# Down weights of experts 3 to 30 as one transfer of 4 MB, on one buffer that is waited for and freed as a whole

## The reference, cut to what matters

```python
def expert_block(args):
    xb, e = args                                   # a block of tokens of expert e
    h = xb @ w_gu[e] + b_gu[e]                     # (1024, 2048) weights: 8 MB
    h_glu = jnp.minimum(h[:, :D_EXPERT], SWIGLU_LIMIT)
    h_lin = jnp.clip(h[:, D_EXPERT:], -SWIGLU_LIMIT, SWIGLU_LIMIT)
    act = h_glu * jax.nn.sigmoid(SWIGLU_ALPHA * h_glu) * (h_lin + 1.0)
    return act @ w_dn[e] + b_dn[e]                 # (1024, 1024) weights: 4 MB
...
return jnp.einsum('tkd,tk->td', y, gates).reshape(bsz, seq, d)
```

## Time and profile before

| | |
|---|---|
| median of the runs | 1021.99 us |
| the profiled execution | 1020.78 us, of which 1019.0 us are its span |
| TensorE (PE) busy | 824.2 us, 81% |
| VectorE busy | 246.4 us, 24% |
| DMA | 421.69 MB, 414 GB/s over the span, about 428 GB/s from 130 us to the end |
| chain that ended last | DMA 56%, PE 36%, VectorE 5% |
| `gu_buf` from `w_gate_up` | 128 transfers of 2048 KB |
| `dn_buf` from `w_down` | 62 transfers of 2048 KB, 2 of 1024 KB |

### The profile page before, as it was taken

How to read it: one execution, slowest core, us unless ns; L and a number is a source line. 1 busy time by engine, 2 the same in 40 slices (tenths; PEclk the granted TensorE clock), 3 DMA queues, 4 the chain that set the end, 5 groups by cost and what they waited for, 6 DMA issues and landing times.

```text
span 1019.0 us, 20186 instructions
## 1 busy us (share of the span) xinstructions
PE 824.2 (81%) x8447; PEld 355.9 (35%) x8448; DVE 246.4 (24%) x692; ACT 79.5 (8%) x184; POOL 7.2 (1%) x25
## 2 busy tenths in 40 slices
PE   9999879898659999985699976666865885965995
PEld 7884433333213334331133421221321332311432
DVE  2473711221112222221112211111111221210233
ACT  1040100000000000000000000000000000000010
POOL 1000000000000000000000000000000000000000
PEclk9999989999899999998799998888989799988989
DMA  9988699999999999999999999999999999999996
GB/s 327 408 355 346 266 425 425 428 428 428 428 429 428 429 428 429 428 429 429 428 429 429 428 428 429 428 429 428 428 430 428 429 429 428 429 428 428 428 428 291
DMA packets 38903, 421.69 MB, mean 414 GB/s; under 512 B 5907, under 2 KB 6347, under 8 KB 14309
## 3 DMA queue, kind: packets, MB, share of 16 engines
q1 hardware_dynamic: 36436, 420.89, 98.0%
q10 hardware_dynamic: 2400, 0.44, 0.2%
q0 software_dynamic: 48, 0.09, 0.0%
HBM read 420.27 MB, written 1.18 MB: 414 GB/s over the span
## 4 chain that ended last, share of the span: by engine, by line
DMA 56%; PE 36%; DVE 5%; issue 2%; SPq 0%; DVEq 0%; POOLq 0%; ACT 0%; POOL 0%
DMA dn_buf<-in_w_down_dram 56%; PE ps L1038 12%; PE ps L1005 12%; PE ps L838 5%; PE ps L886 3%; PE ps L999 2%; PE ps L857 1%; DVE act_t L730 1%; DVE lin L725 1%; DVE lin L728 1%; DVE glu L722 1%; DVE lin L723 1%; DMA gu_buf<-in_w_in_dram 1%; PE ps L918 0%; PE ps L873 0%
## 5 line engine op out<-in xcount | busy, mean ns | idle before, releaser
L1005 PE MATMUL ps<-gu_buf,rows_t 128*32 128x512 f32 x2880 | 363.8, 651 | 102.0 <-DMA gu_buf<-in_w_gate_up_dram 102.0
L1005 PEld LDWEIGHTS ps<-gu_buf,rows_t 128*32 128x32 f32 x2880 | 93.8, 115 | 362.6 <-issue 196.0
L1038 PE MATMUL ps<-dn_buf,act_t 128*32 128x256 f32 x2848 | 171.1, 385 | 52.1 <-DMA dn_buf<-in_w_down_dram 44.1
L722 DVE TENSOR_SCALAR glu<-ps 128x256 f32<-128x256 f32 x45 | 19.1, 425 | 605.2 <-PE ps L1005 605.2
L1038 PEld LDWEIGHTS ps<-dn_buf,act_t 128*32 128x32 f32 x2848 | 87.7, 110 | 123.4 <-DMA dn_buf<-in_w_down_dram 59.2
L999 PE MATMUL ps<-turned,bias_sel 128*32 128x512 f32 x360 | 50.2, 630 | 22.6 <-issue 22.6
L449 ACT ACTIVATE sig<-glu 128x256 f32<-128x256 f32 x45 | 18.8, 417 | 529.1 <-DVE glu L722 529.1
L838 PE MATMUL ps<-turned,gu_buf 128*128 128x256 f32 x256 | 55.7, 379 | 0.0
L979 PE MATMUL ps<-mix,back 32*128 32x256 f32 x720 | 52.2, 404 | 0.5 <-ACT mix L453 0.5
L955 PE MATMUL ps<-xs,onehot 128*32 128x256 f32 x736 | 50.5, 394 | 1.5 <-DVE onehot L709 1.5
L838 PEld LDWEIGHTS ps<-turned,gu_buf 128*128 128x128 f32 x256 | 48.6, 190 | 6.9 <-issue 0.4
(11 more groups left out here) (234 smaller groups left out, 301.6 us busy)
## 6 DMA issues: line engine op xcount, KB each, us to landing
gu_buf<-in_w_gate_up_dram SPq DMA_DIRECT2D x128, 2048.0 KB, 30.2
dn_buf<-in_w_down_dram SPq DMA_DIRECT2D x62, 2048.0 KB, 13.3
gu_buf<-in_w_in_dram SPq DMA_DIRECT2D x4, 2048.0 KB, 18.4
gu_buf<-in_w_out_dram SPq DMA_DIRECT2D x2, 2048.0 KB, 16.9
dn_buf<-in_w_down_dram SPq DMA_DIRECT2D x2, 1024.0 KB, 27.1
xs<-in_x_dram SPq DMA_DIRECT2D x2, 512.0 KB, 5.4
gu_buf<-in_w_in_dram SPq DMA_DIRECT2D x2, 512.0 KB, 6.5
gu_buf<-in_w_in_dram SPq DMA_DIRECT2D x1, 1024.0 KB, 9.6
```

Of the source, the lines that this page charges most:

```text
L722: V.tensor_scalar(glu[:], half(HB, 0), SWIGLU_LIMIT, None, ALU.min).then_inc(S["glu_ok"], 1)
L1005: ins = T.matmul(ps[SLOTS * j:SLOTS * (j + 1), HB, :], rows_t[:, k, :], gu_buf[:, b, k, :].rearrange("p (two n) -> p two n", two=2)[:, :, ...
L1038: ins = T.matmul(ps[SLOTS * j:SLOTS * (j + 1), YB, 0:QF], act_t[:, DK * m + q, :], weights[q][:, QF * j:QF * (j + 1)], start=(m == 0 and q ...
```

## The change

For experts 3 to 30 `stream_dn` waits once, for the second half of the last block of the expert before (`dn_used[DC - 1]`, which is `y_ps`), and issues one transfer for the whole of `dn_buf`: 4 MB, 32 KB per partition. It counts on `dn_in[0]`. On TensorE the first half of the down product waits for that count as before, which now stands for all 4 MB; the second half waits for a count on `dn_in[1]` that has been reached since expert 2 (48), and so no longer waits. The transfers of experts 0 to 2 and 31 are as they were; for expert 31 the count on `dn_in[1]` is a smaller number, since fewer transfers have counted there.

```diff
             def stream_dn(e):
-                used = blocks_before(e)
-                for c in range(DC):
-                    stream_dn_chunk(e, c, used)
+                sp.wait_ge(dn_used[DC - 1], blocks_before(e))
+                sp.dma_start(dn_buf[:].rearrange("p q n -> p (q n)"), dn_src[bass.ds(e, 1)].rearrange("o p r -> p (o r)")).then_inc(dn_in[0], 16)
...
             def pair_of_experts(pair):
                 for b in range(2):
                     e = pair * 2 + b
-                    expert(e, b, (pair + 1) * 16, [down_at(0, e * 16), down_at(1, (e + 1) * 16)])
+                    expert(e, b, (pair + 1) * 16, [down_at(0, e * 16), down_at(1, 48)])
...
             e = E - 2
-            expert(e, 0, 16 * (E // 2), [down_at(0, e * 16), down_at(1, (e + 1) * 16)])
+            expert(e, 0, 16 * (E // 2), [down_at(0, e * 16), down_at(1, 48)])
...
                     elif q == DK:
-                        pe.wait_ge(dn_in[1], 16 * E)
+                        pe.wait_ge(dn_in[1], 64)
```

## The result

The changed kernel takes 1048.51 us (median of 4 runs, 1046.84 to 1049.15), the kernel before on the same chip 1021.94 us. The ratio is 1.0253 (95% interval 1.024 to 1.0266): 26.6 us slower. The forecast was 1033 us with a range up to 1041. The direction was right; of the size the forecast had 11 us.

A forecast was written before the change was run, and what follows sets the result against it. The expert loop was taken as bound by transfer bytes over rate. On the profiled 1020.78 us, +13.3 for the clock and -2.0 for packets gave 1032.1, with the median 1.2 above: 1033 us, range 1021 to 1041.

The forecast's parts named there:

- What bounds the kernel, and where the down weights are issued: Expert loop: transfer bytes over rate, 29.36 us per expert; two-block experts' down issue moves from L + 14.4 to L + 17.9.
- L: The time at which the whole of an expert's down weights has landed; issue times are counted from it.
- The room at full clock: Two-block experts: down issue against the end of the stream in flight, -0.7 to +0.8 us, taken as 0.
- two pieces: Down transfers: issue to first bytes, 0.9 to 1.4 us; last byte to landing, 0 to 1 us.
- rival 3: All 14 two-block experts: issue late at full clock too, room -0.7, 1043 us; chance of above 1037 us 0.14.
- its sign: Transfer queue: gaps also where both experts have two blocks would show the issue late at full clock.
- The Trainium skill's fixed cost of about 2 us: Each DMA transfer: about 2 us beside its bytes; serial it would save 56 us, but taken as overlapped.
- The clock behind the longer wait: TensorE behind one-block experts: half clock after the landing, 1.9 us lost in 7 two-block experts, 13.3 us (0 to 22).
- Larger packets: 28 down transfers with 32 KB per partition, not 16: 2.0 us saved, between 0 and 2.5.
- Fewer issues: SyncE: 28 issues and waits fewer, worth nothing because it waits anyway.

The follow-up runs named there:

- the run with four matmuls: The control with 4 matmuls of 128 x 512 inside its TensorE branch, result not needed: 1036.73 us.
- the control: The changed kernel plus an empty TensorE branch ahead of the act_t wait, taken in the first block behind a one-block expert: 1045.9 us.
- the run with the late release alone: The kernel before, with both 2 MB down transfers issued only when the second half of the expert before is done: 1031.17 us, ratio 1.0077.
- four row groups left out: The changed kernel without four of the eight row groups (k = 0, 2, 4, 6) of the gate and up product: 1027.02 us, ratio 1.0053.

## Why the prediction was wrong, and where right

1. *What bounds the kernel, and where the down weights are issued.* Right. The issue came at L + 17.94 where I said L + 17.9, and at L + 4.0 behind a one-block expert (forecast L + 3.8), with nothing lost there: their periods are 29.29 us.
2. *The room at full clock.* This is the step that failed. I bounded it by -0.7 to +0.8 us from two pieces, issue to first bytes (0.9 to 1.4) and last byte to landing (0 to 1), and took 0, the middle. Measured, it is -0.8 us: 0.65 to 1.0 lost in each of the six clean stages. Both pieces were within their bounds: the first packets start 0.97 us behind the issue, and the last gate and up packet ends at L + 19.1 for a landing at L + 19.55. The missing piece is that the stream doesn't start at full speed: the first packet on each engine takes 1.8 to 2.0 us in the mean and not 1.22. The earlier trace rows had it already, and I read it as full load: a share of 2.59 at 573 GB/s in 0.2 us is seven packets of 16 KB with 1.18 us each, where a full queue has 0.61. From an issue on a queue about to run dry the whole 4 MB land 12.1 to 12.3 us later, in the middle of a full queue they take 9.7 us (29.29 less the 19.6 of the eight gate and up MB): 2.5 us beside the time of the bytes, where the middles of my two pieces add up to 1.65. Fourteen stages times 0.8 are 11.3 of the 15.5 us that the forecast lacked. It was rival 3, with its 1043 us, to which I gave 0.14, and its sign came: gaps also where both experts have two blocks.
3. *The Trainium skill's fixed cost of about 2 us* (DMA: Bandwidth & Descriptors, Anatomy of one DMA). I set it aside because chunks follow each other at 4.9 us in a full queue. That holds in a full queue. In a queue that runs dry the trace shows 12.26 us for 9.7 us of bytes, and the rule is off by half a us. That section of the Trainium skill fits its 2.0 us on transfers that GpSimd issues; here SyncE does. With these 2.0 us, as an estimate, the landing would be at issue + 11.7 and the loss per stage 0.4 us; it pointed the right way, and I used it only for the case in which it doesn't bind.
4. *The clock behind the longer wait.* Right in mechanism and nearly in size: 13.3 us forecast; the run with four matmuls took 10.5 us away from the stages of its control (9.2 in the medians) and 12.9 from those of the changed kernel. It fell behind all seven landings of a two-block expert behind a one-block one, and in this execution behind an eighth (expert 11); that one didn't fall in the control, and why it fell isn't shown: TensorE's wait ahead of it was 1.85 us, and one of 1.96 ahead of expert 9 left the clock full. I had said that there is no such wait behind a two-block expert; there is, 1.2 to 2.0 us. Each dip cost 1.4 to 2.7 us in the issue (L + 19.3 to L + 20.6 instead of L + 17.9), against 1.9 forecast.
5. *Larger packets.* Right: 2.0 us forecast, 28 x 0.07 measured. The queue moved 32404 packets against 36436, 4032 fewer: the 3584 that I named, and 16 small ones of 4 bytes for each of the 28 transfers saved.
6. *Fewer issues.* Nothing forecast; no run separates it from the packets, whose 0.07 us would hold it.

The sum as it came: 14 x 0.8 = 11.3; the clock 15.3, by which the eight issues behind a dip were later than L + 17.93; packets -2.0; and in expert 29 some 1.2 us more than in stages with the same lateness (the issue at L + 20.4 gave a period of 33.87 us, in expert 3 32.59 us). These are 25.8 of the 26.2 us that the periods show. So the clock took 2.0 us more than forecast, 1.6 of it by the eighth dip. Expert 29 lost about a us more in most other runs too, 2.1 us at full clock where others lost 0.7 to 1.4, though not in the kernel before nor with four row groups left out. Its stream starts like the others, but the first and the last of the 16 DMA engines end 2.1 us apart, where the other 13 stages have 0.8 to 1.2. What holds them up there stays open. So does the spread of 0 to 1.1 us in the run with the late release alone: 12 of its stages had the same issue within 0.1 us. The six at L + 16.1, all odd experts, lost 0.3 to 1.1 us, the six at L + 16.2, all even, 0 to 0.4; no run tells why.

## What to carry to other kernels

A loop of landing, computing and the next issue costs nothing only while the issue comes well ahead of the end of the stream: here 5 us ahead was free in the kernel before, 3.2 to 3.4 cost from nothing to 1.4 us, 2.4 again nothing in two stages, 1.6 cost 0.8, and from there on each us costs one. So don't merge transfers, waits or releases on the single buffer whose release is latest, merge them on the buffer that is free long before; here that turned 26.6 us of loss into 3.4 to 4.0 us of gain. And when a wait grows on an engine in such a loop, count its clock as part of the loop.

## What the runs showed that I had not expected

- The first packet on each engine behind a late issue is slow: 1.97 us where the later ones have 1.23.
- The queue's rate sinks behind an issue even when the stream ahead of it is still 3.4 us long: 344 and 262 GB/s in two windows of 1 us, where 428 is normal, with no window empty.
- Taking 0.86 us of work out of TensorE's block gained nothing: the clock (0.92 over the span in the changed kernel, 0.89 in this one) took it back. More work on TensorE, 3.6 us of matmuls whose result nobody reads, made the kernel 9.2 us faster than its control.
